# The last layer norm split between two engines, with the shift vector placed in the output beforehand and the scaled rows added onto it by transfers

## The chip, the cores and the metric

The kernel runs on one core of a Trainium2 chip. A core has five engines that run their own instruction streams and meet at semaphores: TensorE (PE in the profile, its weight loads PEld), VectorE (DVE), ScalarE (ACT), GpSimd (POOL) and SyncE (SP), which mostly issues transfers. Sixteen DMA engines, shared by all queues, move data between the on-chip memory SBUF and the DRAM (HBM). The metric is device time in microseconds (us) of one launch. A change of 0.2% is 2.3 us.

## The reference, cut to what matters

The program is one layer of a hybrid decoder (attention beside a state-space scan, then 16 experts of which each token uses two). The change touches only its last line, the second layer norm, over 1024 prompt tokens and 64 sample tokens of width 1024:

```python
def layer_norm(x, g, b):
    xf = x.astype(jnp.float32)
    mu = jnp.mean(xf, -1, keepdims=True)
    var = jnp.mean(jnp.square(xf - mu), -1, keepdims=True)
    return ((xf - mu) * lax.rsqrt(var + LN_EPS) * g + b).astype(x.dtype)

def layer_step(...):
    ...
    x = layer_norm(DN_ALPHA * x + mix, lp['ln1_g'], lp['ln1_b'])
    x = layer_norm(DN_ALPHA * x + moe(x, router_w, router_bias, w_gate, w_up, w_down),
                   lp['ln2_g'], lp['ln2_b'])
```

`g` and `b` have one value for each of the 1024 columns; mean and variance are one value a row (token).

## The kernel before

The whole last stage stands in one function, `experts`. Its first and long part runs the experts: for each block of 128 routed token slots, TensorE multiplies with an expert's weights, which SP (gate and up) and ACT (down) load into the tile `raw`, and which ACT and VectorE split into a high part `whi` and a low part `wlo`. GpSimd gathers each block's rows (`xg<-x1d`) and adds the result rows onto the DRAM tensor `acc` with an indirect, accumulating transfer (`acc<-eyb`), one block at a time. The order of all instructions is written out by hand; nothing is scheduled by a planner. SP's last load of the part is that of an up matrix; after it SP waits until all loads have landed and GpSimd has seen the last accumulate land (`all_added`).

Then comes the last norm, over nine tiles of token rows: `z[0]` to `z[7]` with 128 rows of the prompt, `z[8]` with the 64 sample rows, each 1024 columns wide, in the memory of `raw`, which the weights no longer need.

- SP issues nine loads `z[b] <- acc`, one after the other.
- The statistics of a row come from VectorE (`stats`: two `bn_stats` halves and a `bn_aggr`) or, for the tiles in `ACT_STATS`, from ScalarE (`act_stats`: a Copy pass with an accumulated sum, then a Square pass with an accumulated sum).
- The tiles are handled in the groups of `TOGETHER`. For each group g VectorE adds epsilon (`guard`), ScalarE takes the square root, VectorE the reciprocal (`turn_root`).
- `normalise(b)` then makes two passes on VectorE over the tile, both `scalar_tensor_tensor`, the second waiting for the first: (z - mean) * g, and (that) * rstd + b. In it, mean and rstd are one value a row; `s.lg2` and `s.lb2` are the vectors g and b, repeated on 128 partitions.
- SP waits for each tile's second pass (`biased`) and stores it to `y_prompt` or `y_sample`.

ScalarE's stream after the experts is the root of group 0, of group 1, the statistics of tiles 2 and 3, the root of group 2, and so on. VectorE works through the groups in order, statistics of its own tiles first.

Of the kernel before, what the change touches and what calls it, by code (L numbers as in the profile page):

```python
# [10 lines left out]
ALU = mybir.AluOpType  # L11
ACT = mybir.ActivationFunctionType
AX = mybir.AxisListType

P = 128
# [4 lines left out]
NS = NB_DEC * T_DEC  # L20
N = SEQ + NS
QB = SEQ // P
NBLK = QB + 1
# [32 lines left out]
def rows(b):  # L56

    return P if b < QB else NS


def semaphores(nc, stage):

    taken = []
    stage.callback(nc.all_engine_barrier, sem_only=True)
    stage.callback(lambda: nc.clear_and_free_semaphores(taken))

    def sem(name):
        taken.append(nc.alloc_semaphore(name))
        return taken[-1]

    return sem
# [1750 lines left out]
                ch(ts(s.more_pairs[:, 0:1], nb[0:1, 0:1], 1.0, None, ALU.subtract))  # L1822


TOGETHER = ((0,), (1,), (2, 3), (4, 5), (6, 7, 8))
ACT_STATS = (2, 3, 4, 5, 6, 7)


def expert_weights(io, e, i):

    v = io[("moe_w_gate", "moe_w_up", "moe_w_down")[i]][0].rearrange("e (p k) f -> e p (k f)", p=P)
    return v[bass.ds(e, 1), :, :].rearrange("o p n -> p (o n)")


def experts(nc, io, s):
# [6 lines left out]
    with ExitStack() as c:  # L1842
        sb = lambda n, sh, dt=F32: c.enter_context(nc.sbuf_tensor(n, sh, dt))
        sem = semaphores(nc, c)
# [25 lines left out]
        z = [s.raw[:, b * D:(b + 1) * D] for b in range(NBLK)]  # L1870
        cst, mv = sb("cst", [P, 2, 6]), sb("cmv", [P, NBLK, 5])
        warm = sb("warm", [P, 1])
        mean, var, rstd, part = (mv[:, :, k] for k in range(4))
        all_added, loads_in, cseq, mean_made, act_var, var_ready, rooted, weighted, biased, o_out = (
            sem("co_" + n) for n in "all_added loads_in seq mean act_var var rooted weighted biased o_out".split())
        z_in = [sem(f"co_z{b}") for b in range(NBLK)]

        def over_blocks(eng, block):
# [15 lines left out]
        def from_block(b, n):  # L1894

            return type(b) is not int or b >= n
# [4 lines left out]
        with nc.Block() as block:  # L1901
            @block.sync
            def _(sp):
                for i in range(2):
                    sp.sem_inc(w_in[i], 16)
                sp.dma_start(s.lg2[:, :], io["ln2_g"].to_broadcast([P, D])).then_inc(l_in, 16)
                sp.dma_start(s.lb2[:, :], io["ln2_b"].to_broadcast([P, D])).then_inc(l_in, 16)
                with sp.Fori(1, E) as r:
                    e = sp.value_load(s.order[0:1, bass.ds(r, 1)], min_val=0, max_val=E - 1)
                    free = sp.value_load(s.split_by[0:1, bass.ds(r, 1)], min_val=4, max_val=4 * E + 4)  # L1910
                    for i in range(2):
                        sp.wait_ge(w_in[i], 16 * r)
                        sp.wait_ge(lo_made[i], free)
                        sp.dma_start(s.raw[:, slice(*PIECES[i])], expert_weights(io, e, i)).then_inc(w_in[i], 16)

                sp.wait_ge(l_in, 32)
                for i in range(2):
                    sp.wait_ge(w_in[i], 16 * E)


                sp.wait_ge(loads_in, 1)
                sp.wait_ge(all_added, 1)
                for b in range(NBLK):
                    r = rows(b)
                    sp.dma_start(z[b][0:r, :], s.acc[b * P:b * P + r, :]).then_inc(z_in[b], 16)
                for b in range(NBLK):
                    r = rows(b)
                    sp.wait_ge(biased, b + 1)
                    dst = io["y_prompt"][0, b * P:(b + 1) * P, :] if b < QB else io["y_sample"].rearrange("b t d -> (b t) d")
                    sp.dma_start(dst, z[b][0:r, :]).then_inc(o_out, 16)  # L1930
                sp.wait_ge(o_out, 16 * NBLK)

            @block.gpsimd
            def _(pool):
                def gather(b, j):
                    nc.gpsimd.tensor_copy(idxc[j][:, :], s.held[:, bass.ds(b, 1)]).then_inc(idx_kept, 1)
                    pool.wait_ge(idx_kept, b + 1)
                    pool.sem_inc(gather_next, 1)
                    pool.wait_ge(idx_kept, 1)
                    nc.gpsimd.indirect_dma_start(xg[j][:, :], None, s.x1d,  # L1940
                                                 bass.IndirectOffsetOnAxis(ap=idxc[j][:, 0:1], axis=0)) \
                        .then_inc(gathered[j], 16)

                def add_rows(b, j):

                    if from_block(b, 1):
                        pool.wait_ge(added, 16 * b)
                    nc.gpsimd.tensor_copy(gcol[:, :], s.slot_gate[:, bass.ds(b, 1)]).then_inc(slots_kept, 1)
                    nc.gpsimd.tensor_copy(idxs[:, :], s.held[:, bass.ds(b, 1)]).then_inc(slots_kept, 1)
                    pool.wait_ge(slots_kept, 2 * b + 2)  # L1950
                    pool.wait_ge(y_kept, b + 1)
                    pool.sem_inc(add_next, 1)
                    pool.wait_ge(slots_kept, 2)
                    nc.gpsimd.indirect_dma_start(s.acc, bass.IndirectOffsetOnAxis(ap=idxs[:, 0:1], axis=0),  # L1954
                                                 yb[j][:, :], None, compute_op=ALU.add).then_inc(added, 16)

                pool.sem_inc(idx_kept, 2)

                def block_(b, j, loads):
                    pool.wait_ge(x_turned, b + 1)  # L1960
                    gather(b + 2, j)
                    if from_block(b, 1):
                        add_rows(b - 1, 1 - j)

                more = over_blocks(pool, block_)
                add_rows(2 * more + 2, 0)
                pool.wait_ge(added, 32 * more + 48)
                pool.wait_ge(gathered[0], 16 * more + 48)
                pool.wait_ge(gathered[1], 16 * more + 32)
                pool.sem_inc(all_added, 1)  # L1970

            @block.tensor
            def _(pe):
# [63 lines left out]
            def _(act):  # L2037
# [82 lines left out]
                def act_stats(b):  # L2120

                    act.wait_ge(z_in[b], 16)
                    junk = yb[1][:, :]
                    n = ACT_STATS.index(b) + 1
                    if n > 1:
# [6 lines left out]

                for g, some in enumerate(TOGETHER):
                    for b in some:
                        if b in ACT_STATS:
                            act_stats(b)
                    at = slice(some[0], some[-1] + 1)
                    act.wait_ge(var_ready, g + 1)
                    nc.scalar.activation(var[:, at], var[:, at], ACT.Sqrt).then_inc(rooted, 1)

            @block.vector
            def _(dve):
# [52 lines left out]
                def stats(b):  # L2195
                    r = rows(b)
                    dve.wait_ge(z_in[b], 16)
                    nc.vector.bn_stats(cst[0:r, 0, :], z[b][0:r, 0:512])
                    ch(nc.vector.bn_stats(cst[0:r, 1, :], z[b][0:r, 512:D]))
                    ch(nc.vector.bn_aggr(mv[0:r, b, 0:2], cst[0:r, :, :].rearrange("p a b -> p (a b)")))  # L2200

                def guard(g):

                    some = TOGETHER[g]
                    at = slice(some[0], some[-1] + 1)
                    mine = [b for b in some if b in ACT_STATS]
                    if mine:
                        dve.wait_ge(act_var, ACT_STATS.index(mine[-1]) + 1)
                    nc.vector.tensor_scalar(var[:, at], var[:, at], EPS / ALPHA ** 2, None, ALU.add).then_inc(var_ready, 1)
# [4 lines left out]
                def turn_root(g):  # L2214
                    some = TOGETHER[g]
                    at = slice(some[0], some[-1] + 1)
                    dve.wait_ge(rooted, g + 1)
                    ch(nc.vector.reciprocal(rstd[:, at], var[:, at]))

                def normalise(b):  # L2220
                    r = rows(b)
                    zb = z[b][0:r, :]
                    nc.vector.scalar_tensor_tensor(zb, zb, mean[0:r, b:b + 1], s.lg2[0:r, :], ALU.subtract, ALU.mult)                         .then_inc(weighted, 1)  # L2223
                    dve.wait_ge(weighted, b + 1)
                    nc.vector.scalar_tensor_tensor(zb, zb, rstd[0:r, b:b + 1], s.lb2[0:r, :], ALU.mult, ALU.add)                         .then_inc(biased, 1)  # L2225

                stats(0)
                guard(0)
                stats(1)
                turn_root(0)  # L2230
                guard(1)
                normalise(0)
                turn_root(1)
                normalise(1)
                for g in range(2, len(TOGETHER)):
                    if g == len(TOGETHER) - 1:
                        stats(QB)
                    guard(g)
                    turn_root(g)
                    for b in TOGETHER[g]:  # L2240
                        normalise(b)


def constants():
# [155 lines left out]
```

## Time and profile before

| | us |
|---|---|
| timed runs, median of 3 (lowest, highest) | 1133.85 (1132.3, 1133.9) |
| the profiled execution's own time | 1130.06 |
| its span, from the first instruction's start to the end | 1128.3 |
| the last expert product is written out by ScalarE at | 1081.24 |
| VectorE begins the last norm's statistics at | 1093.50 |
| VectorE's last pass begins at | 1122.29 |
| the store of `y_sample` is issued at | 1123.60 |

The times in the lower part are positions from the start of the span. The last norm fills the last 45 us of it, in which TensorE does nothing. How the engines' work in that stretch hangs together decides what the change does.

### The profile page before, as it was taken

To read this page: it belongs to the slowest core of one execution; us is meant where nothing else is said; L and a number is where in the kernel's file an instruction comes from. 1 tells how busy PE (TensorE), PEld (TensorE's weight loads), DVE (VectorE), ACT (ScalarE), POOL (GpSimd) and SP (SyncE) were. 2 spreads that over 40 slices of the span, in tenths; PEclk is the share of its full clock that TensorE was granted. 3 is DMA by queue.
4 is the path that set the end of the run, shared out by engine and by line. 5 is a ranking of instruction groups with operands and counts; after the bars stand their busy time and mean duration, and the time that the engine had idled before them with its cause. 6 is when DMAs were issued, how large, how long until landed. Compare 5 with 4: busy or idle time off the path is not lost. (4 is left out here: it accounts for less than half of the span.)

```text
span 1128.3 us, 17858 instructions
## 1 busy us (share of the span) xinstructions
PE 1013.8 (90%) x5490; PEld 829.1 (73%) x5491; DVE 687.6 (61%) x1361; ACT 526.8 (47%) x902; POOL 234.6 (21%) x562
## 2 busy tenths in 40 slices
PE   6999999998999989999962899999999999999920
PEld 5877889788576666788842688888888888888710
DVE  4547558341789528455557656644566798686437
ACT  4233333423687737222231235644465687576324
POOL 0623556900200100000000012222232222213100
PEclk9999999999899999999985899999999999999965
DMA  7130241213750245643211778666878899997355
GB/s 247 58 102 29 76 131 38 70 39 106 253 172 1 64 150 184 249 153 112 103 57 37 299 261 271 208 197 228 288 255 303 287 353 377 340 333 250 105 162 192
DMA packets 52289, 201.34 MB, mean 178 GB/s; under 512 B 10146, under 2 KB 16162, under 8 KB 46082
## 3 DMA queue, kind: packets, MB, share of 16 engines
q1 hardware_dynamic: 41714, 138.43, 34.5%
q0 software_dynamic: 7488, 27.27, 10.3%
q10 hardware_dynamic: 3024, 34.87, 7.9%
q8 instruction: 32, 0.52, 0.2%
q14 instruction: 31, 0.25, 0.1%
HBM read 163.80 MB, written 36.73 MB: 178 GB/s over the span
## 5 line engine op out<-in xcount | busy, mean ns | idle before, releaser
L2149 DVE TENSOR_TENSOR wlo<-raw,whi 128x1024 fp32r<-128x1024 f32 x192 | 221.8, 1220 | 35.5 <-ACT whi L2046 34.6
L2046 ACT ACTIVATE whi<-raw 128x1024 fp32r<-128x1024 f32 x184 | 179.3, 1049 | 31.3 <-PE psG L1991 19.5
L1989 PE MATMUL psG<-whi,exs 128*128 128x512 f32 x200 | 82.0, 410 | 7.3 <-DVE wlo L2149 5.3
L1989 PE MATMUL psY<-whi,ehs 128*128 128x512 f32 x200 | 81.0, 405 | 4.3 <-DVE wlo L2149 4.3
L1954 POOL DMA_INDIRECT acc<-eyb,idxs x25 | 41.4, 1654 | 188.8 <-ACT eyb L2064 188.8
L1991 PE MATMUL psG<-whi,exs 128*128 128x512 f32 x200 | 79.2, 396 | 0.0
L1990 PE MATMUL psG<-wlo,exs 128*128 128x512 f32 x200 | 79.2, 396 | 0.0
L1991 PE MATMUL psY<-whi,ehs 128*128 128x512 f32 x200 | 78.7, 393 | 0.0
L1990 PE MATMUL psY<-wlo,ehs 128*128 128x512 f32 x200 | 78.6, 393 | 0.0
L1991 PE MATMUL psU<-whi,exs 128*128 128x512 f32 x200 | 78.1, 390 | 0.0
L1989 PE MATMUL psU<-whi,exs 128*128 128x512 f32 x200 | 77.8, 389 | 0.0
L1990 PE MATMUL psU<-wlo,exs 128*128 128x512 f32 x200 | 77.8, 389 | 0.0
L791 PE MATMUL pa<-xT,wi 128*128 128x288 f32 (+1 forms) x192 | 64.1, 334 | 1.8 <-DVE wi L969 1.8
L2052 ACT ACTIVATE exs<-psX 128x1024 fp32r<-128x1024 f32 x25 | 25.7, 1027 | 80.2 <-PE psX L1978 80.2
L792 PE MATMUL pa<-xT,wi 128*128 128x288 f32 (+1 forms) x192 | 63.0, 328 | 0.0
L793 PE MATMUL pa<-xT,wi 128*128 128x288 f32 (+1 forms) x192 | 63.0, 328 | 0.0
L791 PE MATMUL pa<-wi,xT 128*128 128x512 f32 (+1 forms) x144 | 57.6, 400 | 2.8 <-DVE wi L969 2.8
L1403 PE MATMUL pm<-wo,ap 128*128 128x512 f32 (+1 forms) x144 | 57.5, 399 | 0.7 <-ACT tg L1561 0.7
L1405 PE MATMUL pm<-wo,ap 128*128 128x512 f32 (+1 forms) x144 | 56.3, 391 | 0.0
L793 PE MATMUL pa<-wi,xT 128*128 128x512 f32 (+1 forms) x144 | 56.3, 391 | 0.0
L792 PE MATMUL pa<-wi,xT 128*128 128x512 f32 (+1 forms) x144 | 56.2, 390 | 0.0
L1404 PE MATMUL pm<-wo,ap 128*128 128x512 f32 (+1 forms) x144 | 56.1, 390 | 0.0
(410 smaller groups left out, 2297.8 us busy)
## 6 DMA issues: line engine op xcount, KB each, us to landing
raw<-in_moe_w_gate SPq DMA_DIRECT2D x16, 2048.0 KB, 9.3
raw<-in_moe_w_up SPq DMA_DIRECT2D x16, 2048.0 KB, 10.7
raw<-in_moe_w_down ACTq DMA_DIRECT2D x16, 2048.0 KB
early<-in_w_in SPq DMA_DIRECT2D x27, 256.0 KB, 3.3
stg<-in_x_prompt SPq DMA_DIRECT2D x8, 512.0 KB, 4.4
kc<-in_cache_k SPq DMA_DIRECT2D x16, 256.0 KB, 2.9
vc<-in_cache_v SPq DMA_DIRECT2D x16, 256.0 KB, 3.0
mr<-in_w_out SPq DMA_DIRECT2D x8, 512.0 KB, 3.2
```

What stands on the lines that cost most here:

```text
L791: pe.matmul(out, *ops(0, 0), start=(k == 0), stop=False)
L792: pe.matmul(out, *ops(0, 1), start=False, stop=False)
L793: last = pe.matmul(out, *ops(1, 0), start=False, stop=(k == KD - 1))
L1403: pe.matmul(out, hi, wo[0][:, k, cols], start=(k == 0), stop=False)
L1404: pe.matmul(out, hi, wo[1][:, k, cols], start=False, stop=False)
L1405: last = pe.matmul(out, lo, wo[0][:, k, cols], start=False, stop=(k == KD - 1))
L1954: nc.gpsimd.indirect_dma_start(s.acc, bass.IndirectOffsetOnAxis(ap=idxs[:, 0:1], axis=0), yb[j][:, :], None, compute_op=ALU.add).then_inc( ...
L1989: pe.matmul(out, hi, w_hi, start=(k == 0), stop=False)
L1990: pe.matmul(out, hi, w_lo, start=False, stop=False)
L1991: last = pe.matmul(out, lo, w_hi, start=False, stop=(k == steps - 1))
L2046: nc.scalar.activation(whi[:, at], s.raw[:, at], ACT.Copy).then_inc(hi_made[i], 1)
L2149: nc.vector.tensor_tensor(wlo[:, at], s.raw[:, at], whi[:, at].bitcast(F32), ALU.subtract) \
```

## The change

- Before the experts' part is over, SP stores `s.lb2` eight times: each 128-row block of `y_prompt` then holds the shift vector in every row.
- VectorE's second pass is dropped for the eight prompt tiles. What is left, renamed `weigh(b)`, is the first pass.
- ScalarE scales the row instead: `activation(Copy, scale=rstd)` in place on `z[b]`. The scale steps of group g - 1 come in ScalarE's stream right after the root of group g; those of the last two prompt tiles come after the root of the new group 5, which holds the sample tile alone.
- GpSimd, not SP, sends the eight tiles out, with `accum_op=ALU.add`, so that a transfer adds the tile onto the shift vector that lies in DRAM. GpSimd waits for the eight early stores once, and for all of its own eight transfers at the end; SP waits for them as well.
- ScalarE computes the statistics of tiles 2, 3, 4 and 6 only (before: 2 to 7); VectorE takes 0, 1, 5, 7 and 8.
- The sample tile keeps both passes on VectorE, and its plain store by SP.

```diff
-TOGETHER = ((0,), (1,), (2, 3), (4, 5), (6, 7, 8))
-ACT_STATS = (2, 3, 4, 5, 6, 7)
+TOGETHER = ((0,), (1,), (2, 3), (4, 5), (6, 7), (8,))
+ACT_STATS = (2, 3, 4, 6)
...
                 sp.wait_ge(l_in, 32)
+                for b in range(QB):
+                    sp.dma_start(io["y_prompt"][0, b * P:(b + 1) * P, :], s.lb2[:, :]).then_inc(shifts_out, 16)
                 for i in range(2):
                     sp.wait_ge(w_in[i], 16 * E)
...
-                for b in range(NBLK):
-                    r = rows(b)
-                    sp.wait_ge(biased, b + 1)
-                    dst = io["y_prompt"][0, b * P:(b + 1) * P, :] if b < QB else io["y_sample"].rearrange("b t d -> (b t) d")
-                    sp.dma_start(dst, z[b][0:r, :]).then_inc(o_out, 16)
-                sp.wait_ge(o_out, 16 * NBLK)
+                sp.wait_ge(biased, 1)
+                sp.dma_start(io["y_sample"].rearrange("b t d -> (b t) d"), z[QB][0:NS, :]).then_inc(o_out, 16)
+                sp.wait_ge(o_out, 16)
+                sp.wait_ge(y_added, 16 * QB)
...
                 pool.sem_inc(all_added, 1)
+
+                pool.wait_ge(shifts_out, 16 * QB)
+                for b in range(QB):
+                    pool.wait_ge(scaled, b + 1)
+                    pool.dma_start(io["y_prompt"][0, b * P:(b + 1) * P, :], z[b][:, :], accum_op=ALU.add) \
+                        .then_inc(y_added, 16)
+                pool.wait_ge(y_added, 16 * QB)
...
                     nc.scalar.activation(var[:, at], var[:, at], ACT.Sqrt).then_inc(rooted, 1)
+                    if g > 0:
+                        for b in TOGETHER[g - 1]:
+                            act.wait_ge(weighted, b + 1)
+                            nc.scalar.activation(z[b][:, :], z[b][:, :], ACT.Copy, scale=rstd[:, b:b + 1]) \
+                                .then_inc(scaled, 1)
...
-                def normalise(b):
+                def weigh(b):
...
-                    dve.wait_ge(weighted, b + 1)
-                    nc.vector.scalar_tensor_tensor(zb, zb, rstd[0:r, b:b + 1], s.lb2[0:r, :], ALU.mult, ALU.add)                         .then_inc(biased, 1)
...
                 for g in range(2, len(TOGETHER)):
-                    if g == len(TOGETHER) - 1:
-                        stats(QB)
+                    for b in TOGETHER[g]:
+                        if b not in ACT_STATS:
+                            stats(b)
                     guard(g)
                     turn_root(g)
                     for b in TOGETHER[g]:
-                        normalise(b)
+                        weigh(b)
+                zb = z[QB][0:NS, :]
+                dve.wait_ge(weighted, NBLK)
+                nc.vector.scalar_tensor_tensor(zb, zb, rstd[0:NS, QB:NBLK], s.lb2[0:NS, :], ALU.mult, ALU.add) \
+                    .then_inc(biased, 1)
```

The line numbers of the changed kernel differ: what was L1925 (load of a tile) is L1928, the Copy and Square passes of `act_stats` (L2127, L2130) are L2135 and L2138, the root (L2139) is L2147.

The first place is ScalarE's stream in the last norm, from the first two roots on (`cmv` holds mean, variance and reciprocal root of all tiles, `eyb` takes output that nobody reads, `raw` is the tile `z`). Before:

```order
L2139 ACTIVATE cmv<-cmv 128x1 x2
L2127 ACTIVATE eyb,cmv<-raw 128x1024
L2130 ACTIVATE eyb,cmv<-raw,cmv 128x1024
L2127 ACTIVATE eyb,cmv<-raw 128x1024
L2130 ACTIVATE eyb,cmv<-raw,cmv 128x1024
L2139 ACTIVATE cmv<-cmv 128x2
```

Now, to the scale steps of tiles 2 and 3:

```order
L2147 ACTIVATE cmv<-cmv 128x1 x2
L2151 ACTIVATE raw<-raw,cmv 128x1024
L2135 ACTIVATE eyb,cmv<-raw 128x1024
L2138 ACTIVATE eyb,cmv<-raw,cmv 128x1024
L2135 ACTIVATE eyb,cmv<-raw 128x1024
L2138 ACTIVATE eyb,cmv<-raw,cmv 128x1024
L2147 ACTIVATE cmv<-cmv 128x2
L2151 ACTIVATE raw<-raw,cmv 128x1024
L2135 ACTIVATE eyb,cmv<-raw 128x1024
L2138 ACTIVATE eyb,cmv<-raw,cmv 128x1024
L2147 ACTIVATE cmv<-cmv 128x2
L2151 ACTIVATE raw<-raw,cmv 128x1024 x2
```

The scale step of tile 0 stands ahead of the statistics of tiles 2 and 3, that of tile 1 behind them and behind the root of group 2, and those of tiles 2 and 3 behind tile 4's statistics and the root of group 3.

The second place is the end of SP's stream, from the loop over the experts' weights on. Before:

```order
L1914 DMA raw<-in_moe_w_gate 128x4096
L1914 DMA raw<-in_moe_w_up 128x4096
L1908 REGISTER_ALU
L1908 COMPARE_AND_BRANCH
L1925 DMA raw<-acc 128x1024 x8
L1925 DMA raw<-acc 64x1024
L1930 DMA out_y_prompt<-raw 128x1024 x8
L1930 DMA out_y_sample<-raw 64x1024
```

Now:

```order
L1915 DMA raw<-in_moe_w_gate 128x4096
L1915 DMA raw<-in_moe_w_up 128x4096
L1909 REGISTER_ALU
L1909 COMPARE_AND_BRANCH
L1919 DMA out_y_prompt<-lb 128x1024 x8
L1928 DMA raw<-acc 128x1024 x8
L1928 DMA raw<-acc 64x1024
L1930 DMA out_y_sample<-raw 64x1024
```

The eight 512 KB stores of `lb` come behind the last weight load and ahead of the tile loads; the eight stores of finished prompt tiles are gone from SP.

The third place is the end of GpSimd's stream, now:

```order
L1955 DMA acc<-eyb,idxs 1216x1024
L1968 ISA
L1969 ISA
L1970 REGISTER_ALU
L1976 DMA out_y_prompt<-raw 128x1024 x8
```

Before, it ended with the last `acc` accumulate and the three waits; the eight transfers of prompt tiles are new there.

## Rows read from the trace of the kernel before

**Rows 1.** The page's first line: span and instruction count.

```profile
span 1128.3 us, 17858 instructions
```

**Rows 2.** The chain of waits, last stretch: start us, length us, what.

```profile
1081.24 1.12 ACT eyb L2064
...
1083.18 6.23 DMA acc<-eyb,idxs
...
1089.70 3.71 DMA raw<-acc
...
1122.29 1.28 DVE raw L2225
```

**Rows 3.** Timeline, 1094 to 1124 us: start, length, engine, line, operation.

```profile
1095.14 0.69 DVE L2198 BATCH_NORM_STATS2 cst<-raw 128x6 f32<-128x512 f32 x1
...
1096.69 0.16 DVE L2218 RECIPROCAL cmv<-cmv 128x1 f32<-128x1 f32 x1
...
1096.96 1.28 DVE L2223 SCALAR_TENSOR_TENSOR raw<-raw,cmv,lg 128x1024 f32<-128x1024 f32 x1
...
1097.19 1.04 ACT L2127 ACTIVATE eyb<-raw 128x1024 f32<-128x1024 f32 x1
...
1102.19 0.16 DVE L2209 TENSOR_SCALAR cmv<-cmv 128x2 f32<-128x2 f32 x1
...
1102.89 1.28 DVE L2223 SCALAR_TENSOR_TENSOR raw<-raw,cmv,lg 128x1024 f32<-128x1024 f32 x1
...
1104.22 1.28 DVE L2225 SCALAR_TENSOR_TENSOR raw<-raw,cmv,lb 128x1024 f32<-128x1024 f32 x1
...
1105.42 1.28 DVE L2223 SCALAR_TENSOR_TENSOR raw<-raw,cmv,lg 128x1024 f32<-128x1024 f32 x1
...
1123.60 0.49 SPq L1930 DMA_DIRECT2D out_y_sample<-raw  x1
```

**Rows 4.** DMA issues: queue, count, KB each, median us from issue to landing.

```profile
out_y_sample<-raw SPq DMA_DIRECT2D x1, 256.0 KB, 2.9
```

**Rows 5.** GpSimd's accumulates, one row for all: ns min/median/max, first and last start.

```profile
L1954 POOL DMA_INDIRECT acc<-eyb,idxs x25: 1590/1607/2445, 661.2 to 1083.2; - x25
```

**Rows 6.** Timeline of two of GpSimd's transfers, and of VectorE beside one.

```profile
961.61 4.62 DVE L2149 TENSOR_TENSOR wlo<-raw,whi 128x1024 fp32r<-128x1024 f32 x4
...
964.13 2.44 POOL L1954 DMA_INDIRECT acc<-eyb,idxs  x1 [4.67 <-ACT eyb L2064]
...
1055.67 1.00 POOL L1940 DMA_INDIRECT xg<-x1d,idxc  x1 [0.79 <-POOL idxc L1936]
```

**Rows 7.** Windows: stretch, its length, busy us of each engine, clock, DMA share, GB/s.

```profile
1026.00:1034.00 8.00, 8.00 (x42) 6.83 (x41) 1.91 (x2) 1.67 (x2) 0.30 (x2) 1.00 0.95 362
1085.00:1086.00 1.00, 0.00 (x0) 0.00 (x0) 0.00 (x0) 0.00 (x0) 0.00 (x0) 0.50 1.08 86
1086.00:1087.00 1.00, 0.00 (x0) 0.00 (x0) 0.00 (x0) 0.00 (x0) 0.00 (x0) 0.50 0.72 123
1087.00:1088.00 1.00, 0.00 (x0) 0.00 (x0) 0.00 (x0) 0.00 (x0) 0.00 (x0) 0.50 1.05 209
1088.00:1089.00 1.00, 0.00 (x0) 0.00 (x0) 0.00 (x0) 0.00 (x0) 0.00 (x0) 0.50 0.56 107
1092.00:1101.00 9.00, 0.00 (x0) 0.00 (x0) 7.22 (x14) 3.97 (x9) 0.00 (x0) 0.50 1.01 403
1099.00:1124.00 25.00, 0.00 (x0) 0.00 (x0) 23.26 (x30) 12.95 (x25) 0.00 (x0) 0.50 0.58 224
```

**Rows 8.** Timeline of several engines near the last weight loads, 1017 to 1052 us.

```profile
1017.69 0.33 SPq L1914 DMA_DIRECT2D raw<-in_moe_w_up  x1
...
1035.11 3.90 ACT L2046 ACTIVATE whi<-raw 128x1024 fp32r<-128x1024 f32 x4 [0.15 <-issue]
...
1046.61 0.69 DVE L2175 SCALAR_TENSOR_TENSOR ehh<-eth,psU 128x512 f32<-128x512 f32 x1
...
1050.87 0.63 PE L2010 MATMUL psH<-identz,ehh 128*128 128x128 f32 x4
```

More of the change, by code:

```diff
@@ L1875, in experts @@
             sem("co_" + n) for n in "all_added loads_in seq mean act_var var rooted weighted biased o_out".split())
+        shifts_out, scaled, y_added = sem("co_shifts_out"), sem("co_scaled"), sem("co_y_added")
         z_in = [sem(f"co_z{b}") for b in range(NBLK)]
@@ L2218, in turn_root @@
                     ch(nc.vector.reciprocal(rstd[:, at], var[:, at]))
-                def normalise(b):
+                def weigh(b):
                     r = rows(b)
                     zb = z[b][0:r, :]
-                    nc.vector.scalar_tensor_tensor(zb, zb, mean[0:r, b:b + 1], s.lg2[0:r, :], ALU.subtract, ALU.mult)                         .then_inc(weighted, 1)
-                    dve.wait_ge(weighted, b + 1)
-                    nc.vector.scalar_tensor_tensor(zb, zb, rstd[0:r, b:b + 1], s.lb2[0:r, :], ALU.mult, ALU.add)                         .then_inc(biased, 1)
+                    nc.vector.scalar_tensor_tensor(zb, zb, mean[0:r, b:b + 1], s.lg2[0:r, :], ALU.subtract, ALU.mult) \
+                        .then_inc(weighted, 1)
                 stats(0)
@@ L2231, in _ @@
                 guard(1)
-                normalise(0)
+                weigh(0)
                 turn_root(1)
-                normalise(1)
+                weigh(1)
                 for g in range(2, len(TOGETHER)):
-                    if g == len(TOGETHER) - 1:
-                        stats(QB)
+                    for b in TOGETHER[g]:
+                        if b not in ACT_STATS:
+                            stats(b)
                     guard(g)
```

## The prediction

> **What bounds the kernel now.** I read three views in this order. The chain of waits says what the end hangs on: the last expert rows leave ScalarE at 1081.24, their accumulate onto `acc` lands, the first tile is loaded at 1089.70, and from there on the chain is VectorE's up to its last pass at 1122.29 [rows 2]. The reader is to see that nothing but the last norm stands behind 1089.70, and that the span ends at 1128.3 [rows 1]. The windows say how full the engines are in that stretch: of the 25 us from 1099 to 1124 VectorE is busy for 23.26, ScalarE for 12.95, and the DMA engines for 58% [rows 7]. So VectorE's passes are the bound, and anything taken off VectorE counts, until ScalarE, GpSimd's queue or the DMA engines are the bound in its place. The timeline has the single costs [rows 3].
>
> The end after VectorE: its last pass begins at 1122.29, takes 1.28, the store of `y_sample` is issued at 1123.60 and lands 2.9 later [rows 2 to 4], at 1126.5. From the last landing to the end of the span there are 1.8 us (1128.3 - 1126.5). I keep this 1.8 in every case.
>
> **The change, part by part.**
>
> *Costs of one step* [rows 3]. Statistics of a tile on VectorE: 1.55 (1095.14 to 1096.69). A pass that waits for the one before: 1.33 (1102.89 to 1104.22); one that doesn't: 1.20 (1104.22 to 1105.42). From the end of ScalarE's statistics to the first pass, through guard, root and reciprocal: 0.7 (1102.19 to 1102.89). Two tiles' statistics on ScalarE: 5.0 (1097.19 to 1102.19), so 2.5 each. The new scale step is a Copy over 128x1024 on ScalarE; the nearest row is the Copy of the statistics, 1.04.
>
> *The engines.* Up to the first pass on tile 0, 1096.96, nothing changes. It ends at 1098.24, so ScalarE scales tile 0 from 1098.3 to 1099.35, ahead of the statistics of tiles 2 and 3. Those then end at 1104.3, 2.1 later than now. VectorE is done with tile 1 at 1099.65 and stands idle until 1104.3: that is where most of its saved time goes. Tile 1, weighed at 1099.65, is scaled only behind the root of group 2, until 1105.7. VectorE weighs tiles 2 and 3 from 1105.0 to 1107.5 and has tile 5's statistics at 1109.0; ScalarE has tile 4's at 1108.2. Behind the next root ScalarE scales tile 2 until 1110.4, tile 3 until 1111.4, and has tile 6's statistics at 1113.9. VectorE weighs tiles 4 and 5 until 1112.2, has tile 7's statistics at 1113.7. Behind the root of group 4 (1114.1) tiles 4 and 5 are scaled until 1115.3 and 1116.3. VectorE weighs tiles 6 and 7 until 1117.1 and has tile 8's statistics at 1118.6; behind that last root tiles 6 and 7 are scaled until 1119.9 and 1120.9, and VectorE's two passes over tile 8 end at 1121.9. So the engines end 1.7 us earlier than now (1123.57), not the 8 x 1.3 = 10 us that the dropped passes took: statistics of 5 and 7 came to VectorE, and each group now waits for ScalarE.
>
> *The accumulates.* A prompt tile now leaves through GpSimd as an accumulate of 512 KB onto DRAM. The trace has one of the same size alone, the last onto `acc`. ScalarE's write ends at 1082.36 (1081.24 + 1.12), GpSimd's instruction begins at 1083.18 and takes 1.59, the least of the 25 [rows 2, 5], and its first packets are at 1085.35, in the first window with data [rows 7]: 3.0 us from the producer's end to the first byte. The four windows from 1085 to 1089 hold it all: 86, 123, 209 and 107 GB/s, together 525 KB; in full swing it moves 209 GB/s at a DMA share of 1.05 [rows 7]. The tile loads move 403 GB/s at 1.01. An accumulate thus keeps all 16 engines busy for 524 KB / 209 = 2.5 us where a plain transfer of it takes 1.3. Other than now, where stores left the DMA engines 42% idle, the train of eight needs 20 us.
>
> Tiles 0 and 1 are out before it matters. Tiles 2 to 7 arrive faster than the DMA engines take them: six in 10.5 us (1110.4 to 1120.9) against 15. So the end hangs on tile 2: 1110.4 + 3.0 + 0.7 (the slow start: 86 and 123 GB/s in the first two windows) + 6 x 2.5 = 1129.1. The sample's store, 256 KB at 403, falls among them and takes 0.6 of the same engines: 1129.7. With the 1.8 behind it the span is 1131.4, **3.1 us longer**.
>
> *Unknown costs, from both sides.* GpSimd's instruction for a transfer without a list of rows stands nowhere in this trace. The gather's is 1.00, the accumulate's 1.59 alone, and 2.44 beside VectorE's subtraction of two tiles from SBUF, which covers it [rows 5, 6]; VectorE's passes are of that kind. I take 1.59, the same transfer to the same memory. At 1.00 and without the 0.8 ahead of it, the end is 1.4 earlier (+1.7); at 2.44 for the first alone 0.85 later (+4.0). A bubble between queued accumulates, or none of the 0.7: -0.7 to +1.
>
> *The early stores.* Eight times 512 KB go behind the up load issued at 1017.69 [rows 8], 4.2 MB or 10.4 us at 403 GB/s, while the DMA engines are 95% busy from 1026 to 1034 [rows 7] with the last down matrix. I cost them at nothing. Shared half and half, the down load's 2 MB (5 us alone) would land 4 to 5 us later, and ScalarE begins to split it at 1035.11, with TensorE's need for what ScalarE and VectorE do next at 1050.87, when `ehh` has been there since 1047.3 (1046.61 + 0.69) [rows 8]. That cover is 3.6 us, the next weights come later still, and nothing else of SP's queue waits. If it is too thin: at most about +1. GpSimd's wait for these stores is long over by 1099.
>
> A rule of the Trainium skill (DMA: Bandwidth & Descriptors, section Anatomy of one DMA — SWDGE (gpsimd) path) prices a transfer from GpSimd at 2.0 us plus its bytes at 436 GB/s. By it a tile takes an estimated 3.2 us and queued tiles 1.2 each, so DMA would not be the bound, the sample's landing at 1124.8 would be last, and the span 1.7 shorter. The rows of the one accumulate speak against it: 209 GB/s at full share.
>
> **The rivals.**
>
> *Queued accumulates move like plain transfers.* The 209 GB/s is from one transfer alone, and several queued might hide each other's reads; the share of 1.05 speaks against it. At 1.3 us a tile the last scale step decides: 1120.9 + 3.0 + 0.7 + 1.3 = 1125.9, span 1127.7, 0.6 shorter: 1133.2, no change. It decides if a tile takes under about 2.2 us (six in 13), where the sum falls to +1.3. This is the side of the skill's rule above; even its 1.7 shorter is within what can be told from no change.
>
> *GpSimd's issue becomes the bound.* If each instruction takes 2.44 beside VectorE's passes, with the 0.8 ahead of it, GpSimd gives out a tile in 3.25, more than the 2.5 of the DMA engines. From tile 2 at 1110.4 the last begins at 1126.7, its data 3.8 later at 1130.5, then 0.7 + 2.5 + 0.6: 1134.2, span 1136.0: 7.7 longer, 1141.5. For it: VectorE is nearly always in a two-input pass there. Against: half of the 25 accumulates took at most 1.61 [rows 5], though VectorE is busy in the experts' part as well. The Trainium skill (SBUF — State Buffer, section SBUF: two separate sides) calls the port pair that VectorE and GpSimd share an exclusive lock, held for a whole instruction, which a VectorE operation with two SBUF inputs takes against a GpSimd operation that reads SBUF; the 2.44 looks like it, once.
>
> *The early stores hold up the experts:* +1 on top of the forecast, 1138.
>
> **How the numbers follow.** The profiled execution took 1130.06 for its span of 1128.3, the timed runs 1133.85 in the median; the difference is carried over, 1133.85 + 3.1 = 1137.0. What can be told from no change is 0.2%, 2.3 us: 1131.6 to 1136.1. The forecast (DMA engines bound the train) has 0.68, from 1135.4 to 1138.5; the first rival 0.13, mostly no change; GpSimd's issue 0.13; the early stores 0.06. Of the forecast's chance 0.2 lies under 1136.1. Slower: 0.48 + 0.13 + 0.06 = 0.67. Same: 0.20 + 0.08 = 0.28. Faster: 0.05, if accumulates and GpSimd are both quick. The range 1133.0 to 1140.0 leaves out the faster cases and most of the second rival.
>
> **What would show it.** Right: VectorE idle about 4.7 us ahead of group 2; tile 1's scale step behind two statistics; DMA share near 1 at some 210 GB/s from 1113 to 1129; the chain ending in an accumulate and no longer in VectorE; `y_sample` issued near 1121.9. Wrong: rates near 400 GB/s in that stretch (first rival); gaps in it, with GpSimd's instructions back to back (second); a later last accumulate onto `acc` than 1083.18 (third). The prediction fails most simply if the order of ScalarE's steps costs other than the 2.1 and 4.7 us worked out here.

## The result, and the profile after

The changed kernel took 1141.13 us (median of 5 runs, 1139.27 to 1143.15) against 1133.85: the ratio is 1.0073, with a 95% interval from 1.0052 to 1.0095. It is slower by 6 to 11 us, where 3.1 was forecast. The profiled execution took 1140.24 us, its span is 1138.5.

The chain of waits of the changed kernel (start us, length us, what) has the same joints as [rows 2] up to the first tile's load:

```profile
1082.16 1.12 ACT eyb L2072
...
1084.10 6.34 DMA acc<-eyb,idxs
...
1090.73 3.53 DMA raw<-acc
...
1105.13 0.18 DVE cmv L2222
...
1122.12 0.85 POOL out_y_prompt L1976
```

It ends in GpSimd's last transfer, no longer in VectorE. The last accumulate onto `acc` starts 0.9 later than before, and that is not the change's: SyncE's last weight load, ahead of the first early store, was already issued 1.0 later (1018.73 against 1017.69 [rows 8]). In the ten profiled executions of this document that accumulate started between 1083.2 and 1088.6; the earliest had a mean granted clock of 0.950, the two latest 0.943. So from here on I count from that accumulate's start: before, 1128.3 - 1083.2 = 45.1 us to the end of the span; now 1138.5 - 1084.1 = 54.4, **9.3 more**.

The timeline of the changed kernel shows the engines' part much as worked out:

```profile
1099.12 1.15 ACT L2151 ACTIVATE raw<-raw,cmv 128x1024 f32<-128x1024 f32 x1 [0.99 <-DVE raw L2236]
...
1105.13 0.17 DVE L2222 TENSOR_SCALAR cmv<-cmv 128x2 f32<-128x2 f32 x1 [4.65 <-ACT eyb L2138]
...
1110.11 2.17 ACT L2151 ACTIVATE raw<-raw,cmv 128x1024 f32<-128x1024 f32 x2
...
1111.54 0.85 POOL L1976 DMA_DIRECT2D out_y_prompt<-raw  x1 [3.80 <-ACT raw L2151]
...
1119.65 2.17 ACT L2151 ACTIVATE raw<-raw,cmv 128x1024 f32<-128x1024 f32 x2
...
1121.29 1.28 DVE L2257 SCALAR_TENSOR_TENSOR raw<-raw,cmv,lb 64x1024 f32<-64x1024 f32 x1
...
1122.60 0.48 SPq L1930 DMA_DIRECT2D out_y_sample<-raw  x1
```

The reader is to see VectorE's idle 4.65 us ahead of group 2: it waits there for ScalarE's statistics of tiles 2 and 3, which stand behind the scale step of tile 0 (1099.12). And the sample's store is issued at 1122.60, 38.5 behind the accumulate, against 40.4 before [rows 3].

The windows from 1105 to the end (stretch, length, busy time of PE, PEld, DVE, ACT, POOL, clock, DMA share, GB/s):

```profile
1105.00:1108.00 3.00, 0.00 (x0) 0.00 (x0) 2.56 (x5) 2.73 (x7) 0.86 (x1) 0.50 0.33 64
...
1114.00:1129.00 15.00, 0.00 (x0) 0.00 (x0) 7.52 (x14) 5.16 (x8) 3.40 (x4) 0.50 1.06 203
1129.00:1132.00 3.00, 0.00 (x0) 0.00 (x0) 0.00 (x0) 0.00 (x0) 0.00 (x0) 0.50 0.46 93
...
1132.20:1138.50 6.30, 0.00 (x0) 0.00 (x0) 0.00 (x0) 0.00 (x0) 0.00 (x0) 0.50 0.00 0
```

From 1114 to 1129 the DMA engines are full, at 203 GB/s, close to the 209 of the single accumulate's best window [rows 7]. The last row is the one that nobody had reckoned with: for 6.3 us nothing moves and no engine counts as busy. SyncE's waits in the same stretch say where it stands:

```profile
SPq L1932 <- DMA out_y_prompt<-raw: 9.1, 1, 9.1
SPq L1902 <- PEq L1902: 4.9, 1, 4.9
```

L1932 is the wait for the eight accumulates: 1123.1 + 9.1 = 1132.2, the last landing. L1902 is the end of the block, where all engines meet; the view names TensorE's sequencer, which had been done for 55 us. It was another. Each engine has a drain instruction on leaving a block. It is not counted as busy and stands in none of the views; the trace's own records have it. Those of TensorE, ScalarE and VectorE end here within 0.1 us of the engine's last work. GpSimd's does not (start us, duration ns):

```
before  1089.67  4144  GpSimd DRAIN
after   1132.37  4802  GpSimd DRAIN
```

Before, GpSimd left the block as soon as the last rows were in `acc`, and its drain lay under the tile loads. Now it leaves behind its last accumulate, and its drain, to 1137.17, is nearly the end of the kernel. That it has to do with transfers, the same trace of before suggests: in the four earlier blocks in which GpSimd issued none, its drain ended within 0.2 us of its last instruction (at 225.5, 301.8, 390.6 and 424.4).

### The profile page after: what moved, and what is told of

Read it like the earlier page. It is cut to its first block and busy times, and to the rows that moved or that the text cites. A ratio compares the mean times of both kernels' runs of the same rounds, so it can differ in the third digit from the quotient of the medians.

```text
span 1138.5 us, 17869 instructions
## 1 busy us (share of the span) xinstructions
PE 1015.8 (89%) x5490; PEld 832.0 (73%) x5491; DVE 680.0 (60%) x1361; ACT 530.5 (47%) x903; POOL 240.8 (21%) x570
## 5 line engine op out<-in xcount | busy, mean ns | idle before, releaser
L2162 DVE TENSOR_TENSOR wlo<-raw,whi 128x1024 fp32r<-128x1024 f32 x192 | 221.6, 1219 | 38.7 <-ACT whi L2054 37.8
L791 PE MATMUL pa<-wi,xT 128*128 128x512 f32 (+1 forms) x144 | 58.7, 407 | 1.3 <-DVE wi L969 1.3
L792 PE MATMUL pa<-wi,xT 128*128 128x512 f32 (+1 forms) x144 | 57.4, 398 | 0.0
L793 PE MATMUL pa<-wi,xT 128*128 128x512 f32 (+1 forms) x144 | 57.3, 398 | 0.0
```

The costliest lines, as they stand in the source:

```text
L791: pe.matmul(out, *ops(0, 0), start=(k == 0), stop=False)
L792: pe.matmul(out, *ops(0, 1), start=False, stop=False)
L793: last = pe.matmul(out, *ops(1, 0), start=False, stop=(k == KD - 1))
L2162: nc.vector.tensor_tensor(wlo[:, at], s.raw[:, at], whi[:, at].bitcast(F32), ALU.subtract) \
```

## The experiments

For every run the table has the time against runs of the kernel before on the same chip, and the tail: span minus start of the last accumulate onto `acc`, in the profiled execution. The ratio is estimated from all runs and can differ by 0.1% from the quotient of the medians. Each tail is from one execution. How well such stretches repeat is seen where the engines do the same: from the accumulate to the issue of the sample's store it took 38.3 to 38.7 us in the changed kernel, e2, e3, e4 and e5, and 40.4 and 40.1 in the kernel before and e1. So I read nothing from less than 0.5 us of a tail.

| run | median us | before, same chip | ratio, 95% interval | tail us |
|---|---|---|---|---|
| kernel before | 1133.85 | | | 45.1 |
| changed kernel | 1141.13 | 1133.85 | 1.0073 (1.0052 to 1.0095) | 54.4 |
| e1: before, GpSimd waits for the stores | 1138.08 | 1133.70 | 1.0031 (1.0013 to 1.0049) | 48.9 |
| e2: changed, GpSimd doesn't wait | 1141.38 | 1133.70 | 1.0057 (1.0034 to 1.0079) | 52.0 |
| e3: changed, plain transfers | 1138.85 | 1133.70 | 1.0037 (1.0019 to 1.0054) | 49.6 |
| e4: changed, no early stores | 1142.38 | 1132.31 | 1.0092 (1.0069 to 1.0115) | 53.9 |
| e5: changed, SyncE stores plainly | 1131.29 | 1133.70 | 0.9981 (0.9960 to 1.0001) | 43.8 |
| e6: mix, four tiles the new way | 1132.20 | 1132.31 | 0.9996 (0.9982 to 1.0010) | 43.1 |
| e7: mix, GpSimd waits for the stores | 1135.62 | 1132.31 | 1.0033 (1.0020 to 1.0046) | 47.9 |
| e8: mix, five tiles | 1132.07 | 1133.65 | 0.9997 (0.9982 to 1.0012) | 44.8 |

The theory: of the 9.3 us, 4.5 are GpSimd's drain, now behind everything (the stretch from the last landing to the end: 6.3 against 1.8), and the rest is the train of accumulates, each 2.6 us of all DMA engines (524 KB at 203 GB/s). The rivals: the drain is long only because accumulates had just been in flight; or the engines' new order, or the early stores, cost the time.

**e1, the drain alone.** The kernel before, with one line more; nothing else moves.

```diff
                 pool.sem_inc(all_added, 1)
+                pool.wait_ge(o_out, 16 * NBLK)
```

> The kernel before, with one wait more: GpSimd waits at its stream's end until all nine output stores have landed; it moves nothing. Theory 1 (GpSimd, when it leaves the block after having issued transfers in it, drains for over 4 us, whatever it did last; in the kernel before that lies hidden under the last norm): the drain now starts at the last landing, so the span and the time grow by about 4 us, to 1138, with a gap of 5 to 6 us between last landing and end. Rival (the drain is long only where accumulates were in flight shortly before it): same time as before, 1133.9.

SyncE's waits at the end of e1:

```profile
SPq L1901 <- DMA out_y_sample<-raw: 2.4, 1, 2.4
SPq L1901 <- PEq L1901: 4.3, 1, 4.3
```

The second of them in the kernel before:

```profile
SPq L1901 <- PEq L1901: 0.2, 1, 0.2
```

The tail grew by 3.8, the ratio is 1.0031, and the time is the 1138 expected. GpSimd's drain took 4144 ns, as long as in the kernel before, 37 us after its last transfer had landed. So it isn't about accumulates in flight, and that rival falls: leaving this block cost GpSimd 4.1 us 37 us after its last landing as it did right behind it.

**e2, an earlier drain.** The changed kernel without GpSimd's last wait.

```diff
                         .then_inc(y_added, 16)
-                pool.wait_ge(y_added, 16 * QB)
```

> The changed kernel without GpSimd's own wait for its eight accumulates; SyncE still waits for them all. Theory 1: the drain starts when the last accumulate is issued, about 1123, and is over by the time that the last one lands, so the time falls by 4 to 4.5 us, to 1136.5 to 1137. Rival (the drain itself waits until GpSimd's transfers have landed and then takes its 4.8 us): no change, 1141.

```profile
SPq L1932 <- DMA out_y_prompt<-raw: 9.1, 1, 9.1
SPq L1902 <- PEq L1902: 2.4, 1, 2.4
```

Neither theory had it: the wait at the block's end fell from 4.9 to 2.4, the tail by 2.3. The drain began at 1126.80, with the last issue, lasted 12.5 us, and ended 2.4 behind the last landing (1136.89). It can start early and saves half its price, but it does not end ahead of GpSimd's own transfers. The runs don't decide on the 2.3: the ratio is 1.0057 against 1.0073, and the two intervals overlap. The profiled execution had its last accumulate onto `acc` at 1088.6, 4.5 later than the changed kernel's.

**e3, the accumulates alone.** The eight transfers without `accum_op`, so that the shift vector is missing.

```diff
-                    pool.dma_start(io["y_prompt"][0, b * P:(b + 1) * P, :], z[b][:, :], accum_op=ALU.add) \
+                    pool.dma_start(io["y_prompt"][0, b * P:(b + 1) * P, :], z[b][:, :]) \
```

> The changed kernel with GpSimd's eight transfers as plain stores, not accumulates (the shift vector is then missing from the prompt output). Theory 1 with the DMA engines as the bound of the train: at 1.3 instead of 2.5 to 2.7 us a tile the last landing follows the last scale step, 5 to 6 us earlier, and the 4.8 us drain stays: 1135.5. Rival (the train is paced by GpSimd's issue and the scale steps, not by the DMA engines): at most 1.5 us earlier, 1139.5.

The DMA issues of e3 (queue, count, KB, median us to landing), the same row of the changed kernel, and the window of e3 over the train:

```profile
out_y_prompt<-raw POOLq DMA_DIRECT2D x8, 512.0 KB, 3.2
```

```profile
out_y_prompt<-raw POOLq DMA_DIRECT2D x8, 512.0 KB, 6.8
```

```profile
1112.00:1128.00 16.00, 0.00 (x0) 0.00 (x0) 11.19 (x18) 9.01 (x13) 3.19 (x6) 0.50 0.58 212
```

The DMA share of 0.58 stands against 1.06 in the changed kernel: each packet of 4 KB took its DMA engine 162 ns here and 328 ns there (medians of the trace's packet records). The tail fell by 4.8, a little less than the 5 to 6 us expected, and the drain stayed at 4802 ns. That is the accumulates' share of the loss, shown by itself. The time, 1138.85, is not the 1135.5 of the theory, which had been counted from the changed kernel's profiled execution (1140.24); by the ratios, 1.0037 against 1.0073, the gain is some 4 us, well above the rival's 1.5. A plain transfer from GpSimd landed 3.2 us after its issue, and 3.2 is also the estimate by the Trainium skill's rule (DMA: Bandwidth & Descriptors, section Anatomy of one DMA — SWDGE (gpsimd) path); the accumulate's 6.8 in a queue the rule doesn't give.

**e4, the early stores.**

```diff
-                for b in range(QB):
-                    sp.dma_start(io["y_prompt"][0, b * P:(b + 1) * P, :], s.lb2[:, :]).then_inc(shifts_out, 16)
...
-                pool.wait_ge(shifts_out, 16 * QB)
```

> The changed kernel without SyncE's eight early stores of the shift vector and without GpSimd's wait for them (the prompt output is then added onto whatever lay there). Theory (the early stores are hidden in the experts' part, as costed): the same time as the changed kernel, 1141 within 0.2%, and the stretch from the issue of the last up-matrix load to the last accumulate onto acc stays at 65 to 65.5 us. Rival (the stores hold up the experts): 1 us or more comes off that stretch, and off the time.

From the issue of the last up-matrix load to the last accumulate onto `acc` it took 65.9 us here, 65.4 in the changed kernel and 65.5 before. The tail is 0.4 shorter, which is too little to read, and the time isn't shorter. In the changed kernel the packets of the eight stores run from 1027.5 to 1049.5, at a DMA share of 1.01 to 1.04. They did delay the last two loads of down matrices. The one that the prediction priced landed 47.6 us ahead of the last accumulate onto `acc`, against 49.5 before (49.9 in e4), 1.9 later and not the 4 to 5 allowed for. ScalarE waited 1.7 us for it (its split begins at 1037.44) and issued the other 3.1 later than before, which landed 29.1 ahead, against 33.3 before and in e4. Both delays stayed hidden: the accumulate did not come later by them, and the stores cost nothing that shows.

**e5, the split of the passes alone.** The scaled tiles leave by SyncE, plainly (no shift vector), and GpSimd issues nothing. SyncE also waits for the early stores, ahead of its tile loads.

```diff
+                sp.wait_ge(shifts_out, 16 * QB)
...
+                for b in range(QB):
+                    sp.wait_ge(scaled, b + 1)
+                    sp.dma_start(io["y_prompt"][0, b * P:(b + 1) * P, :], z[b][:, :]).then_inc(y_added, 16)
                 sp.wait_ge(biased, 1)
...
-                pool.wait_ge(shifts_out, 16 * QB)
-                for b in range(QB):
-                    pool.wait_ge(scaled, b + 1)
-                    pool.dma_start(io["y_prompt"][0, b * P:(b + 1) * P, :], z[b][:, :], accum_op=ALU.add) \
-                        .then_inc(y_added, 16)
-                pool.wait_ge(y_added, 16 * QB)
```

> The changed kernel with its early stores, but the scaled tiles are stored plainly by SyncE, and GpSimd issues nothing in the last norm (the shift vector is missing from the prompt output). It shows what the split of the passes between VectorE and ScalarE is worth alone. Theory 1: engines end 1.7 us earlier than before, the drain is hidden again: 1132. Rival (the early stores or ScalarE's new steps cost something by themselves): 1134 or more.

```profile
1124.39 0.49 SPq L1934 DMA_DIRECT2D out_y_sample<-raw  x1
```

The sample's store starts 38.7 behind the last accumulate onto `acc` (1085.7), 1.8 earlier than before, where 1.7 was forecast for the engines. The tail is 1.3 shorter; the ratio is 0.9981, and its interval just reaches 1. So the split alone bought 1.3 us in this order, and the way out through GpSimd costs 10.6 on top of it (54.4 - 43.8): 5.8 with plain transfers (e3's 49.6 - 43.8), most of it the drain, and 4.8 more for the addition.

**e6, a mix that hides both.** Four tiles the new way, so that the train is short and GpSimd is through early; five as before; VectorE takes the statistics of tiles 4 and 5 where it stood idle. GpSimd no longer waits for its own accumulates. Of the edit, without the loops that use the new constants:

```diff
-TOGETHER = ((0,), (1,), (2, 3), (4, 5), (6, 7), (8,))
-ACT_STATS = (2, 3, 4, 6)
+TOGETHER = ((0,), (1,), (2, 3), (4, 5), (6, 7, 8))
+ACT_STATS = (2, 3, 6, 7)
+ADDED = (0, 1, 2, 3)
+SCALE_BEHIND = {2: (0, 1), 3: (2, 3)}
+STATS_AHEAD = {2: (4, 5), 4: (8,)}
...
-                pool.wait_ge(y_added, 16 * QB)
...
```

> A mix: tiles 0 to 3 go the new way (shift vector stored early, ScalarE scales, GpSimd accumulates), tiles 4 to 8 keep both passes on VectorE and SyncE's plain store; VectorE takes the statistics of tiles 4 and 5 where the changed kernel has it idle; scale steps stand behind the roots of groups 2 and 3; GpSimd doesn't wait at the end. Theory (the loss of the change is GpSimd's drain behind its last transfer, and the train of accumulates at 2.6 us each): the four accumulates land by 1116 and the drain is over by 1121, both hidden; VectorE ends at 1121.5 to 1122, 2 us earlier than in the kernel before: 1131.8 against 1133.7. Rival (having GpSimd send anything in the last norm costs a drain of 4 us at the end wherever it ends): 1136.

```profile
1126.49 0.49 SPq L1935 DMA_DIRECT2D out_y_sample<-raw  x1
```

```profile
SPq L1905 <- DMA out_y_sample<-raw: 2.3, 1, 2.3
...
SPq L1905 <- PEq L1905: 0.2, 1, 0.2
```

The sample's store starts 38.7 behind the last accumulate onto `acc` (1087.8), and the wait at the block's end is 0.2 again: the drain, begun at 1113.78 and over at 1127.07, is hidden, and the rival (4 us at the end in any case) falls. The tail is 2.0 shorter than before. The accumulates were slower than expected, though: the last landed at 1124.8, 37.0 behind the last accumulate onto `acc`, and not early. Plain stores ran among them, and from 1111 to 1124.5 the DMA share was 1.04. In the timed runs the gain does not show: the ratio is 0.9996, and its interval reaches to 2.0 us faster.

**e7, the drain put back.** The mix, and GpSimd waits for SyncE's stores.

```diff
                         .then_inc(y_added, 16)
+                pool.wait_ge(o_out, 16 * (NBLK - len(ADDED)))
```

> The mix of the run before, with one wait more: GpSimd waits at its end until SyncE's five stores have landed. It moves nothing. Theory 1: the drain begins at that landing, so the end is 4 to 4.8 us later than in the mix: 1136. Rival (the drain has to do with its own transfers' landing only, here long past): the same as the mix.

```profile
SPq L1905 <- PEq L1905: 4.7, 1, 4.7
```

Tail 4.8 longer than the mix, ratio 1.0033 against 0.9996 by the same runs of the kernel before: one wait that moves nothing costs 3.4 us by the medians, and the time is close to the 1136 expected. The wait alone puts the drain back at the end, as in e1, here in another kernel.

**e8, one tile more.** Tile 4 the new way as well, tiles 2 to 5 in one group. Otherwise the edit is that of e6.

```diff
-TOGETHER = ((0,), (1,), (2, 3), (4, 5), (6, 7), (8,))
-ACT_STATS = (2, 3, 4, 6)
+TOGETHER = ((0,), (1,), (2, 3, 4, 5), (6, 7, 8))
+ACT_STATS = (2, 3, 6, 7)
+ADDED = (0, 1, 2, 3, 4)
+SCALE_BEHIND = {2: (0, 1, 2, 3), 3: (4,)}
+STATS_AHEAD = {2: (4, 5), 3: (8,)}
...
```

> The mix with tile 4 on the new way too, and tiles 2 to 5 in one group, so that VectorE saves one pass and one guard and root, and ScalarE does not stand idle between two roots. Theory: VectorE ends 1.1 to 1.2 us earlier than in the mix, 3 us earlier than in the kernel before counted from the last accumulate onto acc; GpSimd's fifth accumulate lands about 36 us behind that accumulate, its drain ends 2.5 to 4 us later, just ahead of the last plain store: 1130.5, 0.25% under the kernel before. Rival (the fifth accumulate is too late, and the drain shows again at the end): the stretch from the last accumulate onto acc to the end is 44 us or more, no gain over the mix.

```profile
1123.09 0.49 SPq L1935 DMA_DIRECT2D out_y_sample<-raw  x1
```

```profile
out_y_sample<-raw SPq DMA_DIRECT2D x1, 256.0 KB, 5.3
```

VectorE ended 1.1 earlier than in the mix (the store starts 37.6 behind the accumulate), but the store then took 5.3 to land instead of 2.9. The fifth accumulate's packets ran beside it until 1126.3, and from 1123.6 to then the DMA share was 1.01. The tail is 44.8, 1.7 longer than the mix, where the rival had 44 or more. The drain has only a small part in it: the wait at the block's end is 0.6. No version here that keeps the shift vector beats the kernel before by what the runs can tell.

## Why the prediction was wrong

The direction held, and the first rival (queued accumulates at the speed of plain transfers) fell: 203 GB/s at a share of 1.06. The size did not: 3.1 forecast, 9.3 by the tails, 7.3 by the medians.

- **The step that failed** is the sentence "From the last landing to the end of the span there are 1.8 us. I keep this 1.8 in every case." It was 6.3 (1138.5 - 1132.2). The 1.8 was read from a kernel in which GpSimd's drain had begun 37 us ahead. What leaving costs GpSimd was not asked, although the change makes it the last to leave. This is 4.5 of the 6.2 missed; e1 and e7 show it alone at 3.8 and 4.8.
- **Landing** came 4.8 later than before, counted from the last accumulate onto `acc` (48.1 against 43.3), for 3.2 forecast (1129.7 - 1126.5; with the 1.8 the prediction's sum is 1131.5, and it writes 1131.4). Two terms were off and partly cancel. The 3.0 from the producer's end to the first byte was 1.7: tile 2 is scaled at 1111.25, the first packets are at 1112.95; GpSimd's direct instruction takes 0.85, not 1.59, and begins 0.3 behind the producer, not 0.8 (1111.54). From there the train with the sample's store took 19.3 and not 16.3 (1112.95 to 1132.2): 203 GB/s over 15 us instead of 209, and a ragged end, 93 GB/s in the last 3 us, at a DMA share of 0.46.
- **The engines** ended as worked out: VectorE idle 4.65 (4.7), sample's store 1.9 earlier (1.7).
- **Early stores** at nothing: right by the time (e4), though not by lying idle beside the loads: ScalarE did wait 1.7 us for a down load, and the experts' part had room for it.
- **The second rival** (GpSimd's issue as the bound) gave 7.7 and so came near the time, for a wrong reason: the eight instructions took 0.85 to 0.96 each, and none was held up beside VectorE. Its 2.44 was one case, and VectorE's subtraction covers most of it and not all: it ends at 966.23, GpSimd's instruction at 966.57 [rows 6].
- **The difference carried over** from the profiled execution: before, it lay 3.8 under the median, after, 0.9. With the same 3.8 the 9.3 would give 1143, at the upper end of the runs' 1139.3 to 1143.2; the median is 2 us less.

Open is why the drain takes what it takes. It was 4144 ns where GpSimd had issued only transfers by a list of rows in the block (before, e1, e5), 4475 with four direct ones on top (e7) and 4802 with eight, accumulating or plain (changed kernel, e3, e4): 82 to 83 ns for each direct transfer. What the 4144 are, no run shows. Open is also why the last accumulates of the train spread so much over the DMA engines.

## What to carry to other kernels

When a change moves an engine's last instruction to the end of a block, ask what that engine does on leaving it, and read it where it is hidden now: views of busy time don't show it, a silent stretch behind the last landing does. Here GpSimd's last transfer should have landed some 3 us before the last landing of all (the drain ended 2.3 us behind it in e6 and e8), with no wait behind it, or it should not be in the last stage. And an accumulate onto DRAM takes the DMA engines twice as long as a store: count it against what they can take from its first tile on, not as a free addition.

## What the runs showed of the hardware

- GpSimd's drain on leaving a block in which it had issued transfers: 4.1 to 4.8 us when its transfers had landed (seven executions), and until 2.6 to 2.8 us behind their last packet when begun ahead of it (e2, e6, e8). That is no fixed rule: in the block ahead of the experts, behind two gathers, it ended 0.4 behind their last packet (619.1, kernel before). In four blocks without transfers it ended within 0.2 us of GpSimd's last instruction.
- An accumulate of SBUF rows onto DRAM in queue: about 200 GB/s at full DMA share, against 403 for loads [rows 7]; 6.8 us to landing in the train against 3.2 for the same transfers without the addition (e3); 328 ns for a packet of 4 KB against 162.
- GpSimd's instruction for a direct accumulate took 0.85 us, for a plain transfer of the same size 0.53 (e3), for an accumulate by a list of rows 1.59 [rows 5].
